# State space groups of a hybrid block: Silus of convolved tiles ahead of the evacuations, head products ahead of the state's product

## What is computed

```python
xbc = silu(causal_dwconv(xbc, conv_w, conv_b))        # 4 taps
xs, bm, cm = split(xbc)                               # 2048, 4 x 128, 4 x 128
dt = softplus(dt_raw + dt_bias); a = -exp(a_log)
# per group g (4), head (8 per group, 64 wide), chunk of 128 positions:
#   h_t = exp(dA_t) h_(t-1) + B_t xdt_t^T ;  y_t = C_t h_t
y = ssd_chunked(xs * dt, dt * a, bm, cm) + xs * d_skip
y = y * silu(z)
y = y * rsqrt(mean(y * y over the group) + eps) * norm_w
```

## Time and profile before

| | us |
|---|---|
| median of 3 runs | 3452.99 |
| lowest, highest | 3450.5, 3461.78 |
| profiled execution | 3452.74 |
| its span | 3450.9 |
| TensorE busy in the span | 3287.2 |
| VectorE busy | 1642.7 |
| ScalarE busy | 1412.2 |

### The profile page before, as it was taken

How to read it: one execution, slowest core, us unless ns; L and a number is a source line. 1 busy time by engine, 2 the same in 40 slices (tenths; PEclk the granted TensorE clock), 3 DMA queues, 4 the chain that set the end, 5 groups by cost and what they waited for, 6 DMA issues and landing times. The chain is left out here.

```text
span 3450.9 us, 41951 instructions
## 1 busy us (share of the span) xinstructions
PE 3287.2 (95%) x15370; PEld 2644.2 (77%) x15370; DVE 1642.7 (48%) x2465; ACT 1412.2 (41%) x2342; POOL 77.5 (2%) x52
## 2 busy tenths in 40 slices
PE   8999999989999999999989999979999999999998
PEld 6888777768888788877777888847777777778886
DVE  3333467753333433346776333366566446343332
ACT  4332436553332433243665332245555347233321
POOL 0001000010001000100001000100000000000000
PEclk9999999999999999999999999989999999999999
DMA  4233250013232233324001233211122222222231
GB/s 139 96 104 101 93 138 20 1 62 102 93 110 83 81 96 102 101 92 136 15 12 62 92 97 114 75 58 57 57 64 67 83 93 86 88 83 97 94 108 67
DMA packets 86024, 286.35 MB, mean 83 GB/s; under 512 B 15856, under 2 KB 19440, under 8 KB 85360
## 3 DMA queue, kind: packets, MB, share of 16 engines
q1 hardware_dynamic: 84336, 282.80, 25.8%
q10 hardware_dynamic: 1536, 1.57, 0.2%
HBM read 269.12 MB, written 2.10 MB: 79 GB/s over the span
## 5 line engine op out<-in xcount | busy, mean ns | idle before, releaser
L326 DVE TENSOR_TENSOR wlo<-raw,whi 128x1024 fp32r<-128x1024 f32 (+3 forms) x464 | 609.1, 1313 | 930.1 <-ACT whi L322 930.0
L361 PE MATMUL ps<-xh,whi 128*128 128x512 f32 x2256 | 884.8, 392 | 12.2 <-DVE wlo L326 6.1
L362 PE MATMUL ps<-xl,whi 128*128 128x512 f32 x2256 | 879.4, 390 | 0.0
L363 PE MATMUL ps<-xh,wlo 128*128 128x512 f32 x2256 | 879.2, 390 | 0.0
L322 ACT ACTIVATE whi<-raw 128x1024 fp32r<-128x1024 f32 (+3 forms) x464 | 515.4, 1111 | 637.2 <-PE ps L363 580.1
L361 PEld LDWEIGHTS ps<-xh,whi 128*128 128x128 f32 x2256 | 424.5, 188 | 109.8 <-issue 20.6
L362 PEld LDWEIGHTS ps<-xl,whi 128*128 128x128 f32 x2256 | 424.4, 188 | 89.0 <-issue 1.7
L363 PEld LDWEIGHTS ps<-xh,wlo 128*128 128x128 f32 x2256 | 424.4, 188 | 88.8
L361 PE MATMUL ps<-ffn_hh,whi 128*128 128x512 f32 x880 | 344.0, 391 | 0.0
L363 PE MATMUL ps<-ffn_hh,wlo 128*128 128x512 f32 x880 | 342.4, 389 | 0.0
L362 PE MATMUL ps<-ffn_hl,whi 128*128 128x512 f32 x880 | 342.4, 389 | 0.0
(11 more groups left out here) (395 smaller groups left out, 4047.2 us busy)
## 6 DMA issues: line engine op xcount, KB each, us to landing
raw<-in_ffn_up SPq DMA_DIRECT2D x216, 512.0 KB, 3.5
raw<-in_ffn_down SPq DMA_DIRECT2D x80, 704.0 KB, 4.1
raw<-in_ssm_in SPq DMA_DIRECT2D x44, 512.0 KB, 3.4
raw<-in_mix_in SPq DMA_DIRECT2D x32, 512.0 KB, 3.6
raw<-in_lru_in SPq DMA_DIRECT2D x20, 512.0 KB, 3.7
raw<-in_mix_out SPq DMA_DIRECT2D x16, 512.0 KB, 3.8
raw<-in_ssm_out SPq DMA_DIRECT2D x16, 512.0 KB, 3.4
raw<-in_lru_out SPq DMA_DIRECT2D x8, 640.0 KB, 3.9
```

The lines of the kernel that those rows point to most:

```text
L326: dve.tensor_tensor(self.core.wlo[:, u % HALF, 0:width], self.core.raw[:, u, 0:width], self.core.whi[:, u % HALF, 0:width].bitcast(F32), A ...
L361: pe.matmul(out, c.whi[:, h, w], xh[:, k0 + k], start=first and k == 0, stop=False)
L362: pe.matmul(out, c.whi[:, h, w], xl[:, k0 + k], start=False, stop=False)
L363: mm = pe.matmul(out, c.wlo[:, h, w], xh[:, k0 + k], start=False, stop=last and k == nk - 1)
```

## The change

Two things, in all four groups. On ScalarE, `silu(k-2)` is issued ahead of `evacuate(k)` instead of `silu(k-3)` behind it, and the last two ahead of `evacuate(6)`. Within a chunk, TensorE issues the head products ahead of S, with S's wait for `xdd_done`, and VectorE computes `xdd` behind the masks' products instead of ahead of `ce`, with the waits for `xdt_done` and `dec_done`.

```diff
--- before.py
+++ after.py
@@ -2022,9 +2022,6 @@
                     if k >= 1:
                         pe.wait_ge(ph["state_done"], k)
                     pe.wait_ge(ph["cb_done"], k + 1)
-                    if k < CH - 1:
-                        pe.wait_ge(ph["xdd_done"], k + 1)
-                        pe.matmul(c.ps[:, 7], bt, xdd[:], start=True, stop=True).then_inc(ph["s_done"], 1)
                     pe.wait_ge(ph["m_done"], 2 * k + 2)
                     pe.wait_ge(ph["ce_done"], 2 * k + 2)
                     if k == 0:
@@ -2037,6 +2034,9 @@
                         pe.matmul(out, xdt[:, h * HD:(h + 1) * HD], lm[:, h], start=True, stop=False)
                         mm = pe.matmul(out, s.state[:, h * HD:(h + 1) * HD], ce[:, h], start=False, stop=True)
                     mm.then_inc(ph["y_done"], 1)
+                    if k < CH - 1:
+                        pe.wait_ge(ph["xdd_done"], k + 1)
+                        pe.matmul(c.ps[:, 7], bt, xdd[:], start=True, stop=True).then_inc(ph["s_done"], 1)
 
 
                 for k in range(7):
@@ -2083,13 +2083,13 @@
                     act.activation(xs[:, k], xs[:, k], ACT.Silu).then_inc(ph["silu_done"], 1)
 
                 for k in range(7):
+                    if k >= 2:
+                        silu(k - 2)
+                    if k == 6:
+                        silu(5)
                     evacuate(k)
                     if k == 1 and g:
                         group_root(c, s, ph, act)
-                    if k >= 3:
-                        silu(k - 3)
-                silu(4)
-                silu(5)
                 for k in range(CH):
                     act.wait_ge(ph["first_done"], k + 1)
                     for b in range(2):
@@ -2166,11 +2166,6 @@
                     heads = "p (h d) -> p h d"
                     dve.tensor_tensor(xdt[:].rearrange(heads, d=HD), c.ps[:, 3].rearrange(heads, d=HD),
                                       dtg[:, k].unsqueeze(2).broadcast_to([P, 8, HD]), ALU.mult).then_inc(ph["xdt_done"], 1)
-                    dve.wait_ge(ph["xdt_done"], k + 1)
-                    dve.wait_ge(ph["dec_done"], 2 * k + 2)
-                    if k < CH - 1:
-                        dve.tensor_tensor(xdd[:].rearrange(heads, d=HD), xdt[:].rearrange(heads, d=HD),
-                                          sm[:, 2].unsqueeze(2).broadcast_to([P, 8, HD]), ALU.mult).then_inc(ph["xdd_done"], 1)
                     for b in range(2):
                         hs = slice(4 * b, 4 * b + 4)
                         dve.wait_ge(ph["e2_done"], 2 * k + b + 1)
@@ -2179,6 +2174,11 @@
                         hs = slice(4 * b, 4 * b + 4)
                         dve.wait_ge(ph["l_done"], 2 * k + b + 1)
                         dve.tensor_tensor(lm[:, hs], lm[:, hs], cb.unsqueeze(1).broadcast_to([P, 4, P]), ALU.mult).then_inc(ph["m_done"], 1)
+                    dve.wait_ge(ph["xdt_done"], k + 1)
+                    dve.wait_ge(ph["dec_done"], 2 * k + 2)
+                    if k < CH - 1:
+                        dve.tensor_tensor(xdd[:].rearrange(heads, d=HD), xdt[:].rearrange(heads, d=HD),
+                                          sm[:, 2].unsqueeze(2).broadcast_to([P, 8, HD]), ALU.mult).then_inc(ph["xdd_done"], 1)
                     ph.lo(dve, (7 + k) // 4, (7 + k) % 4, D, last=k >= 1)
                     if k == CH - 1:
                         square_sum(0)
```

## The result

| | before | after |
|---|---|---|
| median, us | 3452.86 (5 runs) | 3436.71 (5 runs) |
| lowest, highest | 3450.5, 3461.78 | 3434.09, 3438.43 |
| profiled execution, its span | 3452.74, 3450.9 | 3438.28, 3436.5 |
| TensorE busy | 3287.2 | 3284.0 |

The ratio is 0.9948 with a 95% interval of 0.9936 to 0.9960, so 13.8 to 22.1 us were gained. The ratio is not the quotient of the medians, which is 0.9953; taken by itself it stands for 18.0 us. 3434.0 had been forecast, a gain of 18.7.

What follows compares the result with a forecast made beforehand. TensorE, busy 95% of the span, was taken as the bound, so only its holes or slow clock count. Idle 13.0 + clock 6.5 - late weights 0.8 + order 0 = 18.7 us off 3452.7: 3434.0 us, range 3429 to 3441.

Steps and rivals of the forecast that it cites:

- The idle, 13.0 us: TensorE's wait for the last Silu ahead of chunk 0 goes: 3.25 us a group, 3.34 at most, 13.0 in four.
- The clock, 6.5 us: With no hole in front, chunk 0 runs like chunk 1 at clock 1.00: 6.5 us less over four groups.
- ScalarE ready for chunk 0, by 0.25 us: ScalarE finishes cast and table load a quarter of a microsecond before chunk 0's exponentials are due.
- Late weights of project 4, 0.8 us: Groups 1 to 3: table load and Silu 0 delay evacuation 2, then project 4's weights: 0.27 us each, 0.8 lost, upper end.
- The order within a chunk, 0: Head products ahead of S, xdd behind masked products: no change, bounds 1.0 us either way from a 0.08 seam in 12 chunks.
- The sum: Whole kernel: 13.0 + 6.5 - 0.8 + 0 = 18.7 us gained, from 3452.7 to 3434.0 us.
- The clock falling anyway: Rival: TensorE gets 1.2 GHz at chunk 0 for another reason than the hole; 3440.5 us, chance 0.07.
- the state becoming late: Rival: S behind the heads lands after VectorE asks for it, delaying state, masks and next heads; 3458 us, chance 0.02.
- Silus not early enough: Rival: the last Silu ends behind project 6, so TensorE's wait shrinks but stays; 3436 us, chance 0.06.
- A dearer table switch: Rival: ScalarE's table switches cost more in their new places; from 1.36 us more each, 3442.5 us, no change; chance 0.04.

Runs made afterwards that it cites:

- the fill: Five bf16 matmuls of 512 columns, results unused, behind project 11, added to the kernel with Silus 3 to 5 ahead of evacuation 6: 3430.12 us against 3433.55.
- the hole to the low part: Changed kernel plus a TensorE wait ahead of chunk 0 for the low part of the weights that evacuation 6 prepares: 3457.24 us, ratio 1.0015.

## Why the prediction was right, step by step

*The idle, 13.0 us.* Group 0, which has no late weights, went from 35.70 to 32.35 us between evacuation 0 and chunk 0: 3.35, where 3.34 was the stated most and 3.25 was taken. Four times this is 13.4; the three passed semaphore waits cost nothing. Right, 0.4 too small.

*The clock, 6.5 us.* 54.15 became 47.66: 6.49. Two small terms that the sum did not have cancel in it, which is luck: without a wait ahead of it chunk 0 is 0.1 us shorter than chunk 1 (the kernel with the Silus alone gained 6.9 here), and the new order takes these 0.4 us back. That the hole is the cause was argued from chunks 1 to 3 and is now shown by putting a hole back.

*ScalarE ready for chunk 0, by 0.25 us.* It was 0.11 or 0.12, since without a wait ahead of them the first products take 0.38 instead of 0.49 and the exponentials are wanted 0.1 sooner. This margin was the thinnest of the forecast and held in all four groups.

*Late weights of project 4, 0.8 us.* 13.4 less 12.53 is 0.87, 0.28 a group against 0.27 worked out. What had been called the upper end is the value.

*The order within a chunk, 0.* It costs 0.4 in chunks 0, inside the bounds of 1.0, and it lies where they put it: in the seam, the extra time at a change of matmul shape. The reasons held: the masks' product ends at 2344.46 and the heads start at 2345.49; VectorE waits for ScalarE's cast as before, and its sum of the state comes 13.58 us after the chunk's first matmul, where it came after 13.79. The rows of VectorE in chunk 1, beside the earlier trace rows:

```profile
2343.15 1.31 DVE L2176 TENSOR_TENSOR ssm_m<-ssm_m,ssm_first 128x512 f32<-128x512 f32 x2
2344.37 0.68 DVE L2180 TENSOR_TENSOR ssm_xdd<-ssm_xdt,ssm_small 128x512 f32<-128x512 f32 x1
2347.17 1.23 DVE L326 TENSOR_TENSOR wlo<-raw,whi 128x1024 fp32r<-128x1024 f32 x1 [2.12 <-ACT whi L322]
...
2350.07 0.69 DVE L2194 TENSOR_TENSOR ssm_state<-ssm_state,ps 128x512 f32<-128x512 f32 x1
```

S ends at 2348.56, 1.5 us before the sum wants it; 1.8 had been given.

*The sum.* 13.4 + 6.5 - 0.9 is 19.0 us by rows, against 18.7 forecast. The medians of three comparisons show 16.2, 17.0 and 15.8, the ratios 18.0, 20.0 and 17.3. The first pair of profiles, 14.4 us apart, has its own explanation: starts of phases 2.1 longer by the clock, 2.2 more ahead of the groups, 0.5 behind them. That the medians are also 2 to 3 us short is not explained; each interval takes in 19 us. Nor can they tell such a difference: the code ahead of the groups is the same in all thirteen profiled executions and ended between 2278.5 and 2291.0.

*The rivals.* The clock falling anyway, the state becoming late and Silus not early enough are refuted by the windows, by VectorE's rows and by the waits. A dearer table switch is refuted too: behind L1935, the load starts 0.02 after it and the Silu 0.02 after the load. The drain that the Trainium skill adds to a table load ("ScalarE: Activation LUTs", section "What ACT_TABLE_LOAD costs") appears in none of these rows.

## What to carry to other kernels

When an engine's queue holds the last step of a chain behind an evacuation that must wait for the bounding engine, move that step ahead of it, and take from the timeline the one place where it then delays something: here a table load in front of an evacuation, 0.28 us a group, avoidable by moving only the Silus that were late. Count a hole of TensorE with the clock behind it, here 3.3 us of waiting and mostly 1.6 of slower work, and look for the other holes of that size. An order within a chunk that frees a product sooner brings nothing if a waiting engine takes it up at the same moment as before.

## What the runs showed of the hardware

The granted clock after a hole is not the same each time. Behind 1.7 to 1.9 us it fell in one of four chunks, and not behind the longest of them; behind the 2.5 to 3.0 us of the barrier it stayed up at 3 of 30 starts of groups 1 to 3 in the kernels without the fill (5.84 or 5.85 us in place of 7.2 and more), and behind 3.0 to 3.2 us it fell in all twelve chunks 0 (before, with the order alone changed, with the hole to the low part). How long it stays down varies too: ten of those twelve took 13.5 to 13.7 us and two 15.1 to 15.2. Two executions of one kernel can so differ by some us without any wait being different.

The first weight load of a chunk did not go ahead of its turn behind products on 64 columns (it started together with its matmul, both at 2350.93 in the kernel before; 0.49 us for the first two products), nor behind a wait (0.46 to 0.49 at full clock). Behind full-width matmuls it did (at 2347.97 in the changed kernel, 0.43 us ahead of its matmul; 0.38 for the two). With the new order the seam of 0.1 us moves to S and does not go away.
